# Plain up tiles at the start of each feed-forward stage, and where the norm and the combined inputs are made

## The chip, the cores and the metric

The kernel runs on one core of a Trainium2 chip. The time is the device time of one execution in microseconds (us); three runs of the kernel before gave 2069.99, 2070.28 and 2070.32. One more execution was recorded by the hardware profiler, and all rows below are from it.

## The reference

The input x has 512 tokens of 1024 features in float32. Two blocks follow each other. The kernel computes, in this order: feed-forward stage 0, a mixer with two branches of attention, feed-forward stages 1 and 2, a stick-breaking attention with 16 heads, and feed-forward stage 3. (The second layer type of the reference's second block isn't reached: it has one layer.) Each feed-forward stage is

```
x = x + 0.5 * (silu(gate) * up) @ w_out,   [gate, up] = rmsnorm(x, gain) @ w_in,   w_in: 1024 x (2 * 2816)
rmsnorm(x, g) = x * rsqrt(mean(x * x) + 1e-6) * g
```

Ahead of stage 2 the first block's final norm is applied to x as well, so two norms follow each other there.

## The kernel before, in words

Everything lies with features on the 128 partitions and the 512 tokens along a row, so x is 8 tiles of 128x512. A product in float32 is made of three matmuls of a reduced float32 type: each operand is split into hi (rounded) and lo (the remainder), and hi*hi, hi*lo, lo*hi are added in PSUM. The norm's root is left out of the inputs: xn is x times gain, and the root (rstd) multiplies the results.

Weights come in units of 128x1024 (8 pieces of 128x128) into four slots. SyncE loads a unit, ScalarE rounds it (w_hi, `round_weights`, called ahead by `ahead`), GpSimd makes the remainder (w_lo, `rest`), TensorE multiplies (`unit`, lines 689 to 691, 24 matmuls of 512 columns).

A feed-forward stage n (0 to 3) has 22 up tiles F, each of a gate unit and an up unit; tiles 0 to 11 and 12 to 21 are two chunks c, each followed by its down units, whose results VectorE scales and adds to x. An up tile can be made in two ways. Plain: two units, 48 matmuls of 512 columns. In seven products (Strassen's way, over gate/up, the two halves of the features and the two halves of the tokens): 7 products of 12 matmuls of 256 columns (`product`, lines 766 to 768). The seven need sums of weight quarters (`sum_1` to `sum_4` on VectorE, `copy_c` and `copy_a` on ScalarE, through PSUM), their roundings and remainders (`round_7`, `rest_7`), and combined inputs t of xn: `make_t1` with one operation for each of four features' tiles k, `make_t` with three for each of four j, then rounding on ScalarE (`round_t1`, `round_t`) and remainder on VectorE (`split_t1`, `split_t`); xg is x times gain for them. The products' results are added up on VectorE (`add_p6`, `add_p7_p5`, `add_p4`, `add_p3`), gate gets rstd and silu, and h = up * silu is split.

Before, only stage 0 begins with plain tiles, four of them (PLAIN = 4). Its VectorE makes tile 0, then the combined inputs of k = 0 and 1, then tile 1, and so on (`plain_tiles`). Stages 1 to 3 begin with seven products: `tail_7`, run for each residual tile k as it is updated, rounds and splits the input, makes the combined inputs and adds up squares; `first_products` lets TensorE take products 1, 5, 2 and 6 of tile 0 as their inputs come. The norm's mean is made in tile 1's products, and the first two tiles' gates are kept unscaled until rstd is there (`copied_first`). In stage 2 two means and two roots follow each other (`final_norms`), and cycles F = 2 to 9 scale x by the first norm on VectorE (`x_normed`).

Each engine works off its own list in order, and semaphores hold it back. ScalarE makes the roots by a logarithm and an exponential (`inverse_root`), for which its function table is loaded; silu has another table.

## Time and profile before

| | |
|---|---|
| median of 3 runs | 2070.28 us |
| the profiled execution's own time | 2069.08 us |
| its span, first to last instruction | 2067.3 us |
| TensorE busy | 2017.3 us |
| VectorE, ScalarE, GpSimd busy | 1316.1, 1081.8, 1093.6 us |
| mean granted clock of TensorE | 0.991 of 2.4 GHz |

Busy times overlap between engines, and TensorE's is modelled: a matmul is listed with its own duration although the next one starts before it ends, so its pace is read from counts in a window, not from durations. In the rows PE is TensorE (PEld its weight load), DVE is VectorE, ACT is ScalarE, POOL is GpSimd, SP is SyncE.

### The profile page before, as it was taken

What the parts mean: (1) busy time and instruction counts of PE and PEld (TensorE: products, weight loads), DVE (VectorE), ACT (ScalarE), POOL (GpSimd) and SP (SyncE); (2) the same over time, 40 slices, a digit from 0 to 9 for tenths busy, and PEclk for the clock granted to TensorE, in tenths of its full rate; (3) what the DMA queues carried; (4) which work ended last, traced back from release to release, by engine and by line L of the source; (5) the groups of instructions that cost most, each with busy time, mean ns of one, the idle gap of its engine ahead of it and who ended that gap; (6) DMA issues with size and microseconds to landing.
All of it is one profiled execution on the core that took longest, in us unless ns stands there. A gap on an engine that the chain in (4) does not pass through costs nothing. (4 is left out here: it accounts for less than half of the span.)

```text
span 2067.3 us, 33765 instructions
## 1 busy us (share of the span) xinstructions
PE 2017.3 (98%) x12538; PEld 1782.1 (86%) x12538; DVE 1316.1 (64%) x2312; ACT 1081.8 (52%) x1811; POOL 1093.6 (53%) x728
## 2 busy tenths in 40 slices
PE   8999999999999999999997999999999998999999
PEld 6998998777778889989987998998878877998997
DVE  5762665667763578626677872675688868852762
ACT  6652554344443566525556552564677756642651
POOL 1664775433332458647745674675322335864873
PEclk9999999999999999999999999999999998999999
DMA  4233333322121323332331233223344422332323
GB/s 167 82 103 102 103 101 115 135 82 72 63 71 62 102 72 109 102 107 93 103 112 62 93 100 115 85 97 115 114 133 125 134 82 72 104 107 93 107 96 99
DMA packets 69090, 206.23 MB, mean 100 GB/s; under 512 B 8448, under 2 KB 9472, under 8 KB 68928
## 3 DMA queue, kind: packets, MB, share of 16 engines
q1 hardware_dynamic: 67520, 201.29, 30.3%
q10 hardware_dynamic: 1408, 2.78, 0.4%
q8 instruction: 101, 1.65, 0.3%
q14 instruction: 61, 0.50, 0.1%
HBM read 189.49 MB, written 2.10 MB: 93 GB/s over the span
## 5 line engine op out<-in xcount | busy, mean ns | idle before, releaser
L616 POOL TENSOR_TENSOR w_lo<-raw,w_hi 128x1024 fp32r<-128x1024 f32 (+2 forms) x220 | 442.5, 2022 | 640.4 <-ACT w_hi L1258 475.2
L1258 ACT ACTIVATE w_hi<-raw 128x512 fp32r<-128x512 f32 (+2 forms) x478 | 357.7, 753 | 313.7 <-PE ps L691 250.9
L627 POOL TENSOR_TENSOR w_lo<-s,w_hi 128x512 fp32r<-128x512 f32 x252 | 339.0, 1347 | 195.0 <-ACT w_hi L1258 193.3
L766 PE MATMUL ps<-t_hi,w_hi 128*128 128x256 f32 x1344 | 384.9, 286 | 12.2 <-DVE scratch L1944 6.6
L627 POOL TENSOR_TENSOR w_lo<-raw,w_hi 128x512 fp32r<-128x512 f32 x252 | 324.4, 1299 | 123.4 <-ACT w_hi L1258 123.4
L767 PE MATMUL ps<-t_lo,w_hi 128*128 128x256 f32 x1344 | 382.6, 285 | 0.0
L768 PE MATMUL ps<-t_hi,w_lo 128*128 128x256 f32 x1344 | 382.4, 285 | 0.0
L766 PE MATMUL ps<-xn_hi,w_hi 128*128 128x256 f32 x1008 | 287.7, 285 | 24.3 <-POOL w_lo L627 8.5
L767 PE MATMUL ps<-xn_lo,w_hi 128*128 128x256 f32 x1008 | 287.1, 285 | 0.0
L768 PE MATMUL ps<-xn_hi,w_lo 128*128 128x256 f32 x1008 | 287.1, 285 | 0.0
L766 PEld LDWEIGHTS ps<-t_hi,w_hi 128*128 128x128 f32 x1344 | 260.3, 194 | 16.8 <-DVE scratch L1944 8.1
L767 PEld LDWEIGHTS ps<-t_lo,w_hi 128*128 128x128 f32 x1344 | 260.3, 194 | 0.4
L768 PEld LDWEIGHTS ps<-t_hi,w_lo 128*128 128x128 f32 x1344 | 260.3, 194 | 0.0
L689 PE MATMUL ps<-h_hi_main,w_hi 128*128 128x512 f32 x640 | 249.2, 389 | 0.0
L690 PE MATMUL ps<-h_lo_main,w_hi 128*128 128x512 f32 x640 | 249.2, 389 | 0.0
L691 PE MATMUL ps<-h_hi_main,w_lo 128*128 128x512 f32 x640 | 249.0, 389 | 0.0
L689 PE MATMUL ps<-xn_hi,w_hi 128*128 128x512 f32 x552 | 222.4, 403 | 6.7 <-issue 6.7
L766 PEld LDWEIGHTS ps<-xn_hi,w_hi 128*128 128x128 f32 x1008 | 195.2, 194 | 26.2 <-issue 16.5
L691 PE MATMUL ps<-xn_hi,w_lo 128*128 128x512 f32 x552 | 216.2, 392 | 0.0
L690 PE MATMUL ps<-xn_lo,w_hi 128*128 128x512 f32 x552 | 216.1, 391 | 0.0
L1792 DVE SCALAR_TENSOR_TENSOR ps<-ps,rstd 128x512 f32<-128x512 f32 (+1 forms) x65 | 44.8, 689 | 242.8 <-PE ps L691 242.8
L767 PEld LDWEIGHTS ps<-xn_lo,w_hi 128*128 128x128 f32 x1008 | 195.3, 194 | 0.2
(260 smaller groups left out, 3790.1 us busy)
## 6 DMA issues: line engine op xcount, KB each, us to landing
raw<-weights SPq DMA_DIRECT2D x294, 512.0 KB, 3.2
raw<-weights SPq DMA_DIRECT2D x68, 256.0 KB, 2.8
raw<-weights SPq DMA_DIRECT2D x32, 384.0 KB, 3.0
k_hi_twice<-sb_k_hi SPq DMA_DIRECT2D x31, 128.0 KB, 2.3
k_lo_twice<-sb_k_lo SPq DMA_DIRECT2D x31, 128.0 KB, 2.3
x_sb<-x_t SPq DMA_DIRECT2D x8, 256.0 KB, 6.4
bias<-rel ACTq DMA_DIRECT2D x1, 2048.0 KB, 8.8
q_both<-sb_q_hi SPq DMA_DIRECT2D x16, 128.0 KB, 2.2
```

Source lines behind the costliest of these rows:

```text
L616: nc.gpsimd.tensor_tensor(w_lo[s][:, 0:tiles, :], raw[s][:, 0:tiles, :], w_hi[s][:, 0:tiles, :].bitcast(F32), ALU.subtract).then_inc(S["lo ...
L627: nc.gpsimd.tensor_tensor(quad_of(n, i, w_lo), factor(n, F, i, raw, s_sum), quad_of(n, i, w_hi).bitcast(F32), ALU.subtract).then_inc(S["q_ ...
L689: pe.matmul(to, w_hi[s][:, k, :], hi, start=opens, stop=False)
L690: pe.matmul(to, w_hi[s][:, k, :], lo, start=False, stop=False)
L691: last = pe.matmul(to, w_lo[s][:, k, :], hi, start=False, stop=ends)
L766: pe.matmul(to, w[0][:, k, :], hi, start=opens, stop=False, skip_group_check=True)
L767: pe.matmul(to, w[0][:, k, :], lo, start=False, stop=False, skip_group_check=True)
L768: last = pe.matmul(to, w[1][:, k, :], hi, start=False, stop=(k == QUAD - 1), skip_group_check=True)
L1258: return nc.scalar.activation(dst, src, ACT.Copy)
L1792: return nc.vector.scalar_tensor_tensor(dst, p, scalar, q, ALU.mult, ALU.mult)
```

## The change

Stages 1 to 3 now make tiles 0 and 1 plain and tiles 2 to 11 in seven products; stage 0 keeps its four plain tiles. `first_products`, `opening_cycle`, `tail_7`, `update_7`, `copied_first` and the opening in the tail are gone. The tail squares, rounds and splits each residual tile; for k = 0 to 3 it makes the first combined input of each, and for k = 4 and 5 in stages 1 and 2 (T_IN_TAIL) the three others. The rest of the combined inputs is made behind the tail, as is the norm: the mean comes ahead of the last piece of the first plain unit, ScalarE makes rstd right then, and each plain gate is scaled on its way out of PSUM. ScalarE no longer preloads the logarithm's table in the tail. The first seven-product tile's weights are copied, summed and rounded between plain tiles 0 and 1. In stage 0 the combined inputs of k = 0 and 1 are made ahead of the first gate, and the two first gates follow each other. Stage 2's scaling of x moves from the cycles to the first chunk's down tiles. Between the two chunks, ScalarE's roundings of the next first tile are issued together for k = 6.

```diff
-PLAIN = 4
+PLAIN = [4, 2, 2, 2]
+T_IN_TAIL = [0, 2, 2, 0]
...
-    return PLAIN if n == c == 0 else CHUNKS[c][0]
+    return CHUNKS[c][0] if c else PLAIN[n]
...
+def plain_banks(n, F):
+
+    return [(0, 1), (2, 3), (BANK_OF_2, BANK_OF_2 + 1), (2, 3)][F] if n == 0 else [(weights_bank(n), S2_BANK), (2, 3)][F]
...
+            for u in range(up_unit(n, 0, 0), up_unit(n, PLAIN[n], 0)):
+                if u >= NSLOT:
+                    rest(u)
...
-        def first_products(n, F):
-
-
-            t, p = FFN_INPUT[n], PAIR[n, F]
-            before = FFN_RES[n][0]
-            updated(before - 1, 5)
-            pe.wait_ge(S["xn_lo_done"], DT * t + QUAD)
-            product(n, F, 1)
-            pe.wait_ge(S["t1_lo"], QUAD * n + QUAD)
-            updated(before - 1, 6)
-            product(n, F, 5)
-            pe.wait_ge(S["xn_lo_done"], DT * t + DT - 1)
-            pe.wait_ge(S["p1_copied"], p + 1)
-            product(n, F, 2, (0, QUAD - 1))
-            pe.wait_ge(S["t_lo"], QUAD * n + QUAD - 1)
-            product(n, F, 6, (0, QUAD - 1))
-            pe.wait_ge(S["t_lo"], QUAD * n + QUAD)
-            product(n, F, 6, (QUAD - 1, QUAD))
-            pe.wait_ge(S["xn_lo_done"], DT * t + DT)
-            product(n, F, 2, (QUAD - 1, QUAD))
...
+                if F == first and c == 0:
+                    pe.wait_ge(S["gate_scaled"], FT * n + first - 1)
+                    pe.wait_ge(S["t1_lo"], QUAD * (n + 1))
+                elif F == first:
+                    updated(FFN_RES[n][0], 5)
                 else:
-                    if F == first and c == 0:
-                        pe.wait_ge(S["gate_scaled"], 3)
-                        pe.wait_ge(S["t1_lo"], QUAD)
-                    elif F == first:
-                        updated(FFN_RES[n][0], 5)
-                    else:
-                        pe.wait_ge(S["g1_made"], p)
-                    product(n, F, 1)
-                    if n and c == 0 and F == first + 1:
-                        if n == 2:
-                            mean_squares_final()
-                        else:
-                            mean_square(FFN_STAT[n])
-                    if F >= first + 2:
-                        pe.wait_ge(S["c12_made"], p - 1)
-                    elif F == first + 1 and n == c == 0:
-                        pe.wait_ge(S["gate_scaled"], PLAIN)
-                        pe.wait_ge(S["h_made"], PLAIN)
-                    product(n, F, 5)
-                    if F > first:
-                        pe.wait_ge(S["v2_made"], p)
-                        product(n, F - 1, 4)
-                    if F >= first + 2:
-                        pe.wait_ge(S["c21_made"], p - 1)
-                    if F == first and c == 0:
-                        pe.wait_ge(S["t_lo"], QUAD)
-                    if n == 2 and F == 1:
-                        pe.wait_ge(S["m2_copied"], 1)
-                    product(n, F, 6)
-                    pe.wait_ge(S["p1_copied"], p + 1)
-                    product(n, F, 2)
-                    if F > first:
-                        pe.wait_ge(S["c22_made"], p)
-                        product(n, F - 1, 3)
+                    pe.wait_ge(S["g1_made"], p)
+                product(n, F, 1)
+                if F >= first + 2:
+                    pe.wait_ge(S["c12_made"], p - 1)
+                elif F == first + 1 and c == 0:
+                    pe.wait_ge(S["gate_scaled"], FT * n + first)
+                    pe.wait_ge(S["h_made"], FT * n + first)
+                product(n, F, 5)
+                if F > first:
+                    pe.wait_ge(S["v2_made"], p)
+                    product(n, F - 1, 4)
+                if F >= first + 2:
+                    pe.wait_ge(S["c21_made"], p - 1)
+                if F == first and c == 0:
+                    pe.wait_ge(S["t_lo"], QUAD * (n + 1))
+                product(n, F, 6)
...
+        def plain_tiles(n):
+
+            def one(F, g, waits=None, part=None):
+                u = up_unit(n, F, g)
+                unit(u, u % NSLOT, [plain_banks(n, F)[g]] * UK, xn, waits, part=part)
 
             def first_mean(k):
                 if k == 5:
                     mean_square(S_START)
 
-            first_two()
-            unit(2, 2, [2] * UK, xn)
-            unit(3, 3, [3] * UK, xn, first_mean)
-            tile(2, BANK_OF_2)
-            pe.wait_ge(S["gate_scaled"], 2)
-            pe.wait_ge(S["h_made"], 2)
-            tile(3, 2)
+            if n == 0:
+                first_two()
+                one(1, 0)
+                one(1, 1, first_mean)
+                one(2, 0)
+                one(2, 1)
+                pe.wait_ge(S["gate_scaled"], 2)
+                pe.wait_ge(S["h_made"], 2)
+                one(3, 0)
+                one(3, 1)
+                return
+            waits = first_unit_waits(FFN_INPUT[n], FFN_STAT[n])
+            updated(FFN_RES[n][0] - 1, 1)
+            for g, k0, k1 in ((0, 0, UK - 1), (1, 0, 1), (0, UK - 1, UK), (1, 1, UK)):
+                one(0, g, waits if g == 0 else None, (k0, k1))
+            one(1, 0)
+            one(1, 1)
...
+            elif F == PLAIN[n]:
+                act.wait_ge(S["gate_scaled"], FT * n + F - 1)
...
+        def first_weights(n):
+
+            F = PLAIN[n]
+            copy_c(n, F)
+            round_7(n, F, 1)
+            copy_a(n, F)
+            for i in (5, 6, 2):
+                round_7(n, F, i)
+
+        def plain_tiles(n):
+
+            if n == 0:
+                ahead(2)
+                ahead(3)
+                act.preload_act_table_set("natural_log_exp_and_others")
+                round_sums(S_START)
+                ahead(4)
+                for k in range(QUAD):
+                    make_xg(0, k)
+                root_mean_square(S_START)
+                ahead(5)
+                silu(0, 0)
+                silu(0, 1)
+                round_h(0, 0)
+                round_t1(0, 0)
+                round_t(0, 0)
+                round_h(0, 1)
+                for k in range(1, QUAD):
+                    if k == QUAD - 1:
+                        silu(0, 2)
                     round_t1(0, k)
                     round_t(0, k)
-                if F == PLAIN - 2:
-                    copy_c(0, PLAIN)
-                    copy_a(0, PLAIN)
-                    for i in (1, 5, 6, 2):
-                        round_7(0, PLAIN, i)
+                round_h(0, 2)
+                first_weights(0)
+                silu(0, 3)
+                round_h(0, 3)
+                return
+            u = FFN_BASE[n]
+            round_sums(FFN_STAT[n])
+            ahead(u)
+            first_norm(FFN_STAT[n])
+            ahead(u + 1)
+            if n == 2:
+                second_norm()
+            for j in range(T_IN_TAIL[n], QUAD):
+                round_t(n, j)
+            silu(n, 0)
+            round_h(n, 0)
+            first_weights(n)
+            silu(n, 1)
+            round_h(n, 1)
...
-        def tail_7(k, m):
-
-            t, stat, r = FFN_INPUT[m], FFN_STAT[m], FFN_RES[m][0] - 1
-            act.wait_ge(S["x_updated"], DT * r + k + 1)
-            round_input(k, t)
-            if k < QUAD:
-                nc.scalar.activation(xg[:, k, :], X[:, k, :], ACT.Copy, scale=gains[:, t, k:k + 1])\
-                  .then_inc(S["xg_made"], 1)
-                square(k, k % 2, stat, k)
-                round_t1(m, k)
-                return
-            if k == DT - 1:
-                copy_p1(m, 0)
-            round_t(m, k - QUAD)
-            if k == DT - 1:
-                copy_c(m, 1)
-                round_7(m, 1, 1)
-            square(k, k % 2, stat, k)
-            if k == DT - 1:
-                round_7(m, 1, 5)
-                round_sums(stat)
-            elif k == DT - 2 and m < 3:
-                act.preload_act_table_set("natural_log_exp_and_others")
-
         def tail(k, b, r, t, stat):
             act.wait_ge(S["x_updated"], k + (DT * r + 1))
             square(k, b, stat, k)
             round_input(k, t)
+            if t in FFN_INPUT:
+                m = FFN_INPUT.index(t)
+                if k < QUAD:
+                    make_xg(m, k)
+                    round_t1(m, k)
+                elif k < QUAD + T_IN_TAIL[m]:
+                    round_t(m, k - QUAD)
...
+            if t in FFN_INPUT:
+                m = FFN_INPUT.index(t)
+                if k < QUAD:
+                    make_t1(m, k)
+                    split_t1(m, k)
+                elif k < QUAD + T_IN_TAIL[m]:
+                    make_t(m, k - QUAD)
+                    split_t(m, k - QUAD)
...
-            if n == 2 and 2 <= F < 2 + DT:
-                k = F - 2
-                scale_two(X[:, k, :], X[:, k, :], gains[:, G_FINAL, k:k + 1], scratch[:, 6, :])\
-                    .then_inc(S["x_normed"], 1)
...
+        def split_both(k):
+
+            split_t1(0, k)
+            split_t(0, k)
+
+        def plain_tiles(n):
+
+            if n == 0:
+                for k in range(2):
                     make_t1(0, k)
                     make_t(0, k)
-                    split_t1(0, k)
-                    split_t(0, k)
-                if F == PLAIN - 2:
-                    sums_of_first(0, 0)
-                    rest_of_6(0, PLAIN)
+                dve.wait_ge(S["rstd_ready"], S_START + 1)
+                plain_gate(0, 0)
+                plain_gate(0, 1)
+                make_t1(0, 2)
+                make_t(0, 2)
+                plain_h(0, 0)
+                make_t1(0, 3)
+                make_t(0, 3)
+                split_h(0, 0)
+                plain_h(0, 1)
+                split_both(0)
+                split_h(0, 1)
+                split_both(1)
+                split_both(2)
+                plain_gate(0, 2)
+                plain_h(0, 2)
+                split_both(3)
+                split_h(0, 2)
+            else:
+                split_sums(FFN_STAT[n])
+                for j in range(T_IN_TAIL[n], QUAD):
+                    make_t(n, j)
+                if n == 2:
+                    scale_second_mean()
+                for j in range(T_IN_TAIL[n], QUAD):
+                    split_t(n, j)
+                if n == 2:
+                    both_norms()
+                dve.wait_ge(S["rstd_ready"], FFN_STAT[n] + 1)
+                plain_gate(n, 0)
+                plain_h(n, 0)
+                split_h(n, 0)
+            sums_of_first(n, 0)
+            rest_of_6(n, PLAIN[n])
+            plain_gate(n, PLAIN[n] - 1)
+            plain_h(n, PLAIN[n] - 1)
+            split_h(n, PLAIN[n] - 1)
...
+                if n == 2 and c == 0:
+                    scale_two(X[:, k, :], X[:, k, :], gains[:, G_FINAL, k:k + 1], scratch[:, 6, :])\
+                        .then_inc(S["x_normed"], 1)
+                    dve.wait_ge(S["x_normed"], k + 1)
```

## Rows read from the trace of the kernel before

**Rows 1.** The page: the span and the first row of busy times.

```profile
span 2067.3 us, 33765 instructions
...
PE 2017.3 (98%) x12538; PEld 1782.1 (86%) x12538; DVE 1316.1 (64%) x2312; ACT 1081.8 (52%) x1811; POOL 1093.6 (53%) x728
```

**Rows 2.** Busy time in two undisturbed stretches: matmuls (x) of 512, of 256 columns.

```profile
876.00:934.00 58.00, 58.00 (x258) 48.01 (x257) 13.93 (x21) 14.73 (x21) 27.04 (x16) 1.00 0.30 95
936.00:1032.00 96.00, 96.00 (x802) 96.00 (x802) 68.32 (x128) 59.63 (x112) 74.31 (x58) 1.00 0.31 101
```

**Rows 3.** Busy time (x instructions) by window: stages' starts, later cycles of stage 2.

```profile
27.30:63.05 35.75, 26.61 (x106) 21.11 (x106) 20.37 (x37) 17.98 (x28) 9.09 (x6) 0.90 0.18 59
740.78:866.91 126.13, 121.58 (x988) 120.11 (x986) 97.04 (x169) 82.26 (x148) 93.67 (x72) 0.99 0.29 97
1090.36:1233.95 143.59, 125.58 (x989) 122.63 (x988) 118.07 (x186) 84.86 (x155) 92.88 (x72) 0.96 0.25 84
1703.29:1839.73 136.44, 124.70 (x987) 123.37 (x987) 105.79 (x184) 85.16 (x154) 94.62 (x72) 0.94 0.27 89
1137.00:1215.00 78.00, 72.38 (x591) 71.08 (x591) 67.23 (x106) 44.16 (x84) 53.63 (x42) 1.00 0.28 92
```

**Rows 4.** TensorE in order of time: start, us, instruction [idle before, releaser].

```profile
47.17 0.76 PE L689 MATMUL ps<-xn_hi,w_hi 128*128 128x512 f32 x1 [6.70 <-issue]
...
63.05 0.36 PE L766 MATMUL ps<-xn_hi,w_hi 128*128 128x256 f32 x1 [2.45 <-POOL w_lo L627]
...
747.46 0.36 PE L766 MATMUL ps<-xn_hi,w_hi 128*128 128x256 f32 x1 [3.65 <-ACT scratch L1258]
...
1099.47 0.55 PE L766 MATMUL ps<-xn_hi,w_hi 128*128 128x256 f32 x1 [6.08 <-POOL w_lo L627]
...
1123.11 0.39 PE L766 MATMUL ps<-xn_hi,w_hi 128*128 128x256 f32 x1 [3.68 <-DVE scratch L1971]
...
1148.96 0.39 PE L766 MATMUL ps<-t_hi,w_hi 128*128 128x256 f32 x1 [0.94 <-DVE scratch L1944]
...
1708.62 0.58 PE L766 MATMUL ps<-xn_hi,w_hi 128*128 128x256 f32 x1 [5.17 <-DVE x_sb L2190]
```

**Rows 5.** VectorE, then GpSimd, in order of time, from 1132.5 us.

```profile
1134.01 1.59 DVE L1789 TENSOR_TENSOR scratch<-scratch,rstd 128x512 f32<-128x512 f32 x1
...
1135.53 1.78 DVE L1792 SCALAR_TENSOR_TENSOR x_sb<-x_sb,gains,scratch 128x512 f32<-128x512 f32 x1
...
1132.50 2.55 POOL L627 TENSOR_TENSOR w_lo<-raw,w_hi 128x512 fp32r<-128x512 f32 x2
...
1135.02 1.74 POOL L627 TENSOR_TENSOR w_lo<-s,w_hi 128x512 fp32r<-128x512 f32 x1
```

**Rows 6.** The combined inputs' tile: durations min/median/max in ns.

```profile
L2075 DVE SCALAR_TENSOR_TENSOR t_raw<-x_sb,gains,xg x16: 477/820/1878, 37.6 to 1718.3; 128x256 f32<-128x256 f32 x16
```

**Rows 7.** GpSimd, then VectorE, in order of time, in stage 0's start.

```profile
25.49 9.49 POOL L616 TENSOR_TENSOR w_lo<-raw,w_hi 128x1024 fp32r<-128x1024 f32 x4 [25.05 <-DVE sum_lo L1807]
...
28.94 0.69 DVE L1789 TENSOR_TENSOR scratch<-ps,rstd 128x512 f32<-128x512 f32 x1 [3.25 <-ACT rstd L1322]
...
46.37 0.70 DVE L1789 TENSOR_TENSOR ps<-ps,scratch 128x512 f32<-128x512 f32 x1 [1.18 <-issue]
```

**Rows 8.** ScalarE's groups by form: count, busy us, mean ns.

```profile
L1258 ACT ACTIVATE w_hi<-raw 128x1024 fp32r<-128x1024 f32 x126 | 132.0, 1055 | 153.0 <-PE ps L691 136.3 <-DVE ki L2241 8.0 <-PE ps L768 6.7
...
L1357 ACT ACTIVATE scratch<-x_sb 128x512 f32<-128x512 f32 x40 | 24.8, 621 | 29.9 <-DVE x_sb L2124 29.9
```

**Rows 9.** ScalarE and GpSimd in order of time, before stage 3.

```profile
1687.89 0.72 ACT L1365 ACTIVATE xn_hi<-x_sb,gains 128x512 fp32r<-128x512 f32 x1 [0.29 <-DVE x_sb L2190]
...
1687.68 2.41 POOL L616 TENSOR_TENSOR w_lo<-raw,w_hi 128x1024 fp32r<-128x1024 f32 x1 [8.70 <-ACT w_hi L1258]
```

**Rows 10.** ScalarE in order of time: a table load and the next activation.

```profile
1124.41 1.28 ACT L1403 ACT_TABLE_LOAD   x1
1125.82 0.60 ACT L1403 ACTIVATE ps<-scratch 128x512 f32<-128x512 f32 x1
```

254 lines of the change are left out of this document (79 added, 175 removed).

## The prediction

> **What bounds the kernel now.** I read the page's totals first, then busy time by windows, then TensorE's own list in order of time for what it waited for, then VectorE, ScalarE and GpSimd in the same places. The totals: TensorE is busy 2017.3 of 2067.3 us, so 50 us of idle time is all that better ordering could give back, plus what the lower clock after a pause costs [rows 1]. Two undisturbed stretches give its pace: a matmul of 512 columns every 58.00 / 256 = 0.2266 us, one of 256 columns every 96.00 / 800 = 0.1200 us (two of each count only overlap the edges) [rows 2]. A plain up tile is 48 of the first, 10.88 us; a tile in seven products is 84 of the second, 10.08 us.
>
> The windows at the stage starts show where the loss is [rows 3]. From the last matmul before stage 1 to its eleventh tile lie 126.13 us for 984 matmuls (118.08) and two of the norm's mean (0.45): 7.6 us lost. Stage 2: 143.59 for 118.08 and four of the mean (0.91): 24.6 lost. Stage 3: 136.44, 17.9 lost. In stage 0 the window before the first product holds 105 plain matmuls (23.8 us) in 35.75 us: 11.9 lost. That is 62 us, more than the idle time, because the granted clock is 0.90 to 0.99 of 2.4 GHz there: a pause of 3.65 us or more is followed by matmuls at the 1.2 GHz level. TensorE's waits name the places [rows 4]: 6.70 us for stage 0's first two h tiles; in stages 1 to 3 it waits 3.65, 6.08 and 5.17 us in the first tile's products, since VectorE still works off the last residual tiles with their combined inputs; stage 2 waits again for 3.68 us until the two chained roots are through, then 0.94 us in a later cycle, one of seven such waits. These waits understate: the window over such cycles is 78 us for 589 matmuls (70.7 us), 7.3 us lost [rows 3].
>
> **The change part by part.**
>
> *Six tiles from seven products to plain.* Six times 10.88 - 10.08 = +4.8 us of TensorE, always on the path. The Trainium skill ("TensorE: Matmul & The Clock Gate", Back-to-back issue gap) puts the pace at N / 2.4 GHz + 2.5 ns; that would be 10.36 against 9.17 us a tile and +7.1 us, which speaks more against the change. No row shows that pace; the rows decide.
>
> *What the plain tiles can take back.* In the window of stage 1 two tiles become 96 x 0.2266 = 21.8 us and ten stay (816 matmuls, 97.9 us): 119.7 and the mean. Recoverable, the price already paid: 126.13 - 120.1 = 6.0 us in stage 1; 143.59 - 120.6 = 23.0 in stage 2; 136.44 - 120.1 = 16.3 in stage 3; 11.9 in stage 0, which had four plain tiles already and is only reordered. Sum 57.2 us. What is left of the waits comes off that.
>
> *A cost that the waits don't name.* VectorE's operations with two SBUF inputs and GpSimd's take turns. At 1134.01 a VectorE operation lasts 1.59 us, until 0.55 behind the end of GpSimd's pair; GpSimd's next, started at 1135.02, takes 1.74 us and ends 0.55 before the end of VectorE's next, which takes 1.78 [rows 5]. The first operation of a combined input takes 0.48 us alone and up to 1.88 [rows 6]. So each GpSimd operation holds back one such VectorE operation, and an opening with plain units puts four of 2.41 us [rows 9] there. I count this in every stage. It is what the page "SBUF — State Buffer", Two separate sides, of the Trainium skill calls an exclusive lock; no number here is from there.
>
> *Stage 0.* The eight operations of two combined inputs now stand ahead of the first gate. GpSimd is busy from 25.49 to 34.98 with four remainders [rows 7], so four of the eight wait one out each: 27.9, 30.5, 33.3, 36.0, the others by 38.1 us. The first gate, at 28.94 us now, comes at about 38. Then two gates, eight more combined operations (3.6 us), two h multiplies of 0.70 and a split give the second h tile at 45, against 46.37 + 0.70 now. TensorE pauses at 40.5 for 4.7 instead of 6.70 us, and again has some 2.5 us of half clock. The second wait (2.45, for a first weight remainder) goes: gates, sums and roundings come behind the same h tile, but now with 11 us of plain tile to hide them. Residual 7.8, gain 4.1. Were the turns nothing, the first gate would come at 29.5 and the gain would be 11.9; were GpSimd to hold back all eight, the gain would be -2.
>
> *Stage 1.* Two combined inputs stay in the tail, two move behind it. The last residual update meets a free VectorE, the sums are split 5.5 us behind the last matmul, and the mean stands after 22 plain matmuls (5.0 us) and one more of the other unit (0.7): nothing waits. Weight roundings for the first seven-product tile hang on h of tile 0; I get its first remainders at 760.6 and 762.6 us against TensorE's wish at 763.2 and 764.7. Residual 0.4, gain 5.6. Bounds: 6.0, and 2 if the chain comes 4 us late.
>
> *Stage 2.* The tail has the second sum of squares too; the mean waits about 1.0 us. Then both roots chain: two operations of log and exponential, two multiplies, two more. In this chain stand the two remaining combined inputs and two GpSimd operations, and the splits wait behind the second root on ScalarE. First remainder at 1115.5 (wanted at 1114.1), second at 1117.5, and the first cycle's sums then push the seventh product by 1.4. With 1 us for ripples residual 5.5, gain 17.5. The eight scalings of x (1.78 us each in the cycles [rows 5]) move to the down tiles, where VectorE is busy 13.93 of 58 us [rows 2] and a pair of units lasts 8.2 us: hidden. Without that cover they would cost what they do now, some 9 us. Bounds of the stage: 12 to 23.
> The log's table load is no longer preloaded in the tail. A load takes 1.28 us and the next activation starts 0.13 us behind it [rows 10]; the load runs while ScalarE would wait for the mean, so 0 to 1.3 us. The Trainium skill ("ScalarE: Activation LUTs", What ACT_TABLE_LOAD costs) adds a drain of about 1.38 us; that would make stage 2's gain 16.1. Rows 10 show no such gap.
>
> *Stage 3.* This is the weak place. For the first four tiles ScalarE now squares before it rounds, so the combined difference starts later: square 0.62, round 0.72, product as long, difference and its rounding, about 2.65 us a tile from 1687.89 on, plus a weight rounding of 1.05 [rows 8, 9]. The later four go in strict turns of update, square, round, split: 2.65 us too, though they have no combined inputs any more. With one GpSimd operation in the way I get the inputs of tile 5 at 1709.4, tile 6 at 1712.0, the sums at 1715.3. TensorE is free at 1703.3 and can do tiles 0 to 4: it waits 2.5, 2.0 and 1.9 us. Then four combined inputs with their splits (5.6 + 3.6 us, 4.4 of turns) push the first remainders by 2.3 and the seventh product by 1.3, and the half clock costs 2.7. Residual 12.7, gain 3.6. Without the turns it would be 12, with 4 us more of half clock 0.
>
> *Added waits and queues.* ScalarE's first weight copy now waits for a plain gate, and VectorE's second sum for a plain h; behind the one stand the roundings and silu of tile 1, behind the other the remainder, gate and h of tile 1, and TensorE waits for both. That is the chain I followed above; where it is late, I charged it. SyncE's loads for plain units wait for GpSimd's remainder of the slot's unit, not for six products, so each comes earlier; GpSimd has four remainders of 2.41 us ahead of the first 1.3 us one, done some 10 us before it is due.
>
> *The rest* (bank numbers, the opening of the second halves, loads by the up tile's own slot) moves nothing on the path: the second halves open without a wait now, and 3 us of loads lie far ahead.
>
> **Sum.** 4.1 + 5.6 + 17.5 + 3.6 = 30.8 us off the profiled execution's 2069.08 us (span 2067.3): 2038.3. The median is 1.2 us above that execution; within what this rests on I say 2038.
>
> **The rivals.**
> *Fully hidden* (0.2): the turns and the chains all fit under the plain tiles. For it: GpSimd has few operations in an opening. Against it: rows 5. Stage gains 11.9 + 6.0 + 22 + 12 = 52, time 2017.
> *Late weights everywhere* (0.24): the chain gate, silu, h, rounding, sums, rounding, remainder is serial over three engines; in stage 0 it now ends in a 2.45 us wait [rows 4]. If it is 3.5 us longer than I add up at all four places: 14 us less, 2052. Against it: TensorE has 21.8 us of cover in stages 1 to 3.
> *Slower* (0.03): GpSimd's seven operations of an opening (four of 2.41, three of 1.3 us) each hold back a VectorE operation of the one chain on which h, the rounding and the first product hang; 13.5 us a stage, of which I count about 4.5. All of it would be 36 us more, 2074. It decides from 31 us on, 7.7 a stage. Against it: gates, sums and h read PSUM, and the first gate takes 0.69 us beside a busy GpSimd [rows 7].
> *No change* (0.02): the waits only move behind the plain tiles, by the same amounts.
>
> **How the numbers follow.** The forecast has 0.51. I call within 0.2% (4 us) the same, about what a measurement of this kernel can tell. Range 2018 to 2051: from just above the fully hidden case to most of the late weights. Faster 0.95, same 0.02, slower 0.03.
>
> **What would show it.** Right: plain matmuls of the normed input directly behind stages 1 to 3's last residual matmul; no waits of 0.93 us in stage 2's cycles and the x scalings in the down part at about 0.7 us; the pause at 40 us at 4 to 5 us; a first gate near 38 us; short waits near 1705 to 1716. Wrong: the first gate near 30 us (turns cost less there), or TensorE waiting over 4 us at a first seven-product tile. An undisturbed stage 3 would make it about 10 us faster than I say.

## The result, and the profile after

The changed kernel takes 2038.47 us (median of 4 runs, 2038.09 to 2039.64), the kernel before in the same job 2070.30 (4 runs, 2069.99 to 2071.55). The ratio is 0.9846, with a 95% interval from 0.9829 to 0.9863: 31.8 us less, against a forecast of 2038. The profiled execution has a span of 2036.3 us, 31.0 less than before.

The page's totals, which answer to [rows 1]:

```profile
span 2036.3 us, 33055 instructions
...
PE 2014.3 (99%) x12322; PEld 1769.7 (87%) x12322; DVE 1285.5 (63%) x2245; ACT 1068.1 (52%) x1767; POOL 1074.5 (53%) x704
```

TensorE is busy 3.0 us less although six tiles became 0.8 us dearer each: its mean granted clock is 0.996 instead of 0.991 of 2.4 GHz. Its idle time falls from 50.0 to 22.0 us.

The windows that answer to [rows 3]: from the start of the plain tiles to the first product of the first seven-product tile (stage 0), and from where the matmuls before the stage end to its first down matmul (stages 1 to 3):

```profile
27.30:56.48 29.18, 25.82 (x107) 20.91 (x106) 26.27 (x38) 14.83 (x25) 10.65 (x7) 0.94 0.23 73
733.79:855.14 121.35, 120.43 (x915) 116.24 (x914) 89.26 (x151) 76.94 (x134) 87.10 (x64) 1.00 0.30 101
1078.59:1207.40 128.81, 123.46 (x918) 118.03 (x917) 93.31 (x160) 84.69 (x144) 89.06 (x65) 0.99 0.28 95
1676.73:1808.72 131.99, 125.62 (x916) 118.89 (x915) 98.32 (x167) 80.90 (x142) 86.81 (x64) 0.96 0.27 88
```

The lengths were 35.75, 126.13, 143.59 and 136.44 us. So the gains are 6.6 (7.0 up to the first down matmul), 4.8, 14.8 and 4.4 us: 31.0 in all. The forecast had 4.1, 5.6, 17.5 and 3.6.

TensorE's waits in order of time, which answer to [rows 4]:

```profile
43.94 0.76 PE L696 MATMUL ps<-xn_hi,w_hi 128*128 128x512 f32 x1 [3.36 <-issue]
...
740.31 0.47 PE L708 MATMUL ps<-sum_hi,mean_all_r 128*128 128x512 f32 x1 [0.92 <-DVE sum_lo L1789]
...
1080.83 0.47 PE L696 MATMUL ps<-xn_hi,w_hi 128*128 128x512 f32 x1 [2.08 <-issue]
...
1106.92 0.35 PE L770 MATMUL ps<-xn_hi,w_hi 128*128 128x256 f32 x1 [1.54 <-POOL w_lo L633]
...
1115.13 0.39 PE L770 MATMUL ps<-t_hi,w_hi 128*128 128x256 f32 x1 [1.32 <-DVE scratch L1922]
...
1683.78 0.50 PE L696 MATMUL ps<-xn_hi,w_hi 128*128 128x512 f32 x1 [2.80 <-DVE xn_lo L1818]
...
1686.49 0.80 PE L696 MATMUL ps<-xn_hi,w_hi 128*128 128x512 f32 x1 [1.73 <-DVE xn_lo L1818]
...
1716.47 0.39 PE L770 MATMUL ps<-t_hi,w_hi 128*128 128x256 f32 x1 [0.91 <-DVE scratch L1922]
```

What hung on combined inputs before is gone at the first products; no wait of 0.93 us is left in stage 2's cycles, and 80 us of them (1117.0 to 1197.0) hold 669 matmuls at 0.12 us with TensorE never idle. New is the pause of 2.08 us at 1080.83, in front of the first plain unit of stage 2: its weight remainder was made from 1078.38 to 1080.73, late. Stage 3's waits for its normed inputs are the weak place that the prediction named.

Stage 0's start, VectorE, which answers to [rows 7]:

```profile
25.64 2.03 DVE L2056 SCALAR_TENSOR_TENSOR t_raw<-x_sb,gains,xg 128x256 f32<-128x256 f32 x1 [0.47 <-ACT xg L1396]
27.60 2.62 DVE L2070 SCALAR_TENSOR_TENSOR t_raw<-x_sb,gains,xg 128x256 f32<-128x256 f32 x1
...
32.80 2.50 DVE L2075 SCALAR_TENSOR_TENSOR t_raw<-x_sb,gains,t_raw 128x256 f32<-128x256 f32 x1
35.22 0.47 DVE L2056 SCALAR_TENSOR_TENSOR t_raw<-x_sb,gains,xg 128x256 f32<-128x256 f32 x1
...
36.99 1.28 DVE L1771 TENSOR_TENSOR scratch<-ps,rstd 128x512 f32<-128x512 f32 x2
```

and GpSimd beside it:

```profile
24.98 10.04 POOL L622 TENSOR_TENSOR w_lo<-raw,w_hi 128x1024 fp32r<-128x1024 f32 x4 [24.54 <-DVE sum_lo L1789]
```

Four GpSimd operations, four VectorE operations with both inputs in SBUF at 2.0 to 2.6 us, and the fifth at 0.47: one held back by each, as the prediction counted. The two first gates follow at 36.99.

### The profile page after: what moved, and what is told of

The parts are those of the page before. It is cut to its first block and busy times, and to the rows that moved or that the text cites. A ratio compares the mean times of both kernels' runs of the same rounds, so it can differ in the third digit from the quotient of the medians.

```text
span 2036.3 us, 33055 instructions
## 1 busy us (share of the span) xinstructions
PE 2014.3 (99%) x12322; PEld 1769.7 (87%) x12322; DVE 1285.5 (63%) x2245; ACT 1068.1 (52%) x1767; POOL 1074.5 (53%) x704
## 5 line engine op out<-in xcount | busy, mean ns | idle before, releaser
L622 POOL TENSOR_TENSOR w_lo<-raw,w_hi 128x1024 fp32r<-128x1024 f32 (+2 forms) x232 | 471.8, 2043 | 693.0 <-ACT w_hi L1240 528.3
L633 POOL TENSOR_TENSOR w_lo<-s,w_hi 128x512 fp32r<-128x512 f32 x234 | 312.1, 1335 | 184.8 <-ACT w_hi L1240 183.1
L770 PE MATMUL ps<-t_hi,w_hi 128*128 128x256 f32 x1248 | 353.9, 284 | 2.6 <-DVE scratch L1922 2.2
L771 PE MATMUL ps<-t_lo,w_hi 128*128 128x256 f32 x1248 | 353.5, 283 | 0.0
L772 PE MATMUL ps<-t_hi,w_lo 128*128 128x256 f32 x1248 | 353.5, 283 | 0.0
L633 POOL TENSOR_TENSOR w_lo<-raw,w_hi 128x512 fp32r<-128x512 f32 x234 | 301.7, 1303 | 69.0 <-ACT w_hi L1240 68.9
L696 PE MATMUL ps<-xn_hi,w_hi 128*128 128x512 f32 x648 | 262.3, 405 | 10.3 <-issue 5.4
L770 PE MATMUL ps<-xn_hi,w_hi 128*128 128x256 f32 x936 | 265.3, 283 | 1.5 <-POOL w_lo L633 1.5
L698 PE MATMUL ps<-xn_hi,w_lo 128*128 128x512 f32 x648 | 255.3, 394 | 0.0
L697 PE MATMUL ps<-xn_lo,w_hi 128*128 128x512 f32 x648 | 255.3, 394 | 0.0
```

The costliest lines, as they stand in the source:

```text
L622: nc.gpsimd.tensor_tensor(w_lo[s][:, 0:tiles, :], raw[s][:, 0:tiles, :], w_hi[s][:, 0:tiles, :].bitcast(F32), ALU.subtract).then_inc(S["lo ...
L633: nc.gpsimd.tensor_tensor(quad_of(n, i, w_lo), factor(n, F, i, raw, s_sum), quad_of(n, i, w_hi).bitcast(F32), ALU.subtract).then_inc(S["q_ ...
L696: pe.matmul(to, w_hi[s][:, k, :], hi, start=opens, stop=False)
L697: pe.matmul(to, w_hi[s][:, k, :], lo, start=False, stop=False)
L698: last = pe.matmul(to, w_lo[s][:, k, :], hi, start=False, stop=ends)
L770: pe.matmul(to, w[0][:, k, :], hi, start=opens, stop=False, skip_group_check=True)
```

## The experiments

Twelve kernels ran. Their edits are shown shortened, with words for calls and `...` for what is left out. As times differ by a few us, I also read in each trace how late the first down matmul of every stage comes, and take differences: they show at which stage a microsecond went. Stage 0 is up to that matmul; the others are from one such matmul to the next. Executions with the same stage 0 differ there by up to 1.4 us, and in the later stages by 0.1 (0.4 in stage 3). The interval of a ratio is about 3 us wide to either side, more than the 1.4 to 2.4 us by which single edits of the changed kernel move the median; what is said of these rests on the stage times. The traces are one execution each.

| kernel | time, us | ratio to before | stage 0 | to stage 1 | to 2 | to 3 |
|---|---|---|---|---|---|---|
| before | 2070.3 to 2070.8 | 1 | 141.42 | 725.49 | 367.04 | 605.78 |
| changed | 2038.47 | 0.9846 | 134.39 | 720.75 | 352.26 | 601.32 |
| scalings moved (on before) | 2061.88 | 0.9958 [0.9944, 0.9973] | 142.54 | 725.55 | 358.57 | 606.21 |
| stage 0's order (on before) | 2063.14 | 0.9966 [0.9953, 0.9979] | 135.60 | 725.48 | 367.11 | 605.91 |
| table load at the opening | 2039.83 | 0.9856 [0.9841, 0.9870] | 135.18 | 723.35 | 352.55 | 601.29 |
| no combined inputs in the tail | 2040.07 | 0.9855 [0.9840, 0.9870] | 135.83 | 720.71 | 353.49 | 601.35 |
| table load in the tail | 2038.24 | 0.9845 [0.9829, 0.9861] | 134.82 | 720.76 | 351.57 | 601.33 |
| GpSimd held in stage 0 | 2036.69 | 0.9837 [0.9822, 0.9852] | 132.87 | 720.72 | 352.31 | 601.30 |
| gate ahead of the splits | 2036.35 | 0.9836 [0.9821, 0.9850] | 134.95 | 720.70 | 351.13 | 600.48 |
| updates ahead of the tails | 2036.03 | 0.9834 [0.9820, 0.9849] | 135.47 | 720.75 | 352.28 | 599.15 |
| the four edits | 2031.57 | 0.9809 [0.9795, 0.9822] | 132.87 | 720.76 | 350.42 | 598.24 |
| GpSimd held in 2 and 3 too | 2029.11 | 0.9797 [0.9783, 0.9810] | 132.73 | 720.76 | 348.45 | 597.93 |
| tail of 2 emptied | 2029.06 | 0.9797 [0.9783, 0.9810] | 132.99 | 720.67 | 348.96 | 597.21 |
| norm ahead of inputs 2, 3 | 2029.14 | 0.9800 [0.9786, 0.9813] | 132.45 | 720.71 | 348.48 | 597.92 |

### The scalings of x alone, on the kernel before

```
 cycle(n, c, F):
-    if n == 2 and 2 <= F < 2 + DT:
-        scale_two(X[:, F - 2, :], ...).then_inc(S["x_normed"], 1)
 down(n, c):
     for k in range(DT):
+        if n == 2 and c == 0:
+            scale_two(X[:, k, :], ...).then_inc(S["x_normed"], 1)
+            dve.wait_ge(S["x_normed"], k + 1)
         add_down(n, c, k)
```

> The kernel before with one part of the change alone: the eight scalings of x by the final norm leave the seven-product cycles of stage 2 and stand on VectorE ahead of the eight down updates of the same stage's first half. Theory: in the cycles the scaling is what makes TensorE late (eight cycles of 11.27 us against 10.08), in the down part it hides beside the down matmuls; so cycles of 10.1 us, no TensorE waits of 0.93 us left, and 8 x 1.19 = 9.5 us less: 2070.3 - 9.5 = 2060.8. Rival 1 (the waits would have been filled by something else in the cycle, the turns with GpSimd): half of it or less, 2066 or more. Rival 2 (VectorE in the down part is then late with its updates and TensorE waits for a bank): the gain is given back there, about 2070.

Measured: 2061.88, 8.6 us less; 8.5 of them in stage 2. A window of its later cycles, at full pace:

```profile
1129.60:1209.60 80.00, 80.00 (x669) 80.00 (x668) 61.74 (x113) 51.69 (x98) 62.27 (x48) 1.00 0.33 107
```

The group of the scalings, now in the down part (count, busy us, mean ns, idle before):

```profile
L1792 DVE SCALAR_TENSOR_TENSOR x_sb<-x_sb,gains,scratch 128x512 f32<-128x512 f32 x8 | 9.8, 1224 | 0.0
```

The theory holds, a little short (8.5 of 9.5). They last 1.22 us on the mean (0.74 to 2.72), not the 0.7 that the prediction named, and yet cost nothing there: from this down part's first matmul to that of the next lie 166.12 us, as in the kernel before. So 8.5 of stage 2's 14.8 us have nothing to do with plain tiles.

### Stage 0's order alone, on the kernel before

```
+make_t1/make_t of inputs 0 and 1
 wait rstd
-for F in 0..3: gate F, h F, split F, then two combined inputs with splits (F < 2)
+gate 0, gate 1, input 2, h 0, input 3, split h 0, h 1, splits of the inputs, ...
```

> The kernel before with the order of ScalarE and VectorE in stage 0's plain tiles alone taken from the change. The profile after shows the first seven-product matmul of stage 0 at 56.48 us instead of 63.05. Theory: stage 0 is independent of the other stages' change, so the gain is 6.6 us, of which the prediction had 4.1: 2063.7, with a pause of 3.4 us at 44 us and the first gate at 37 us. Rival: part of the 6.6 us comes from something else in the changed kernel (other weights' order, other waits of TensorE), and the reorder alone gives the 4.1 of the prediction: 2066.2.

Measured: 2063.14, 7.3 us less; in the traces stage 0 is 5.8 us shorter than in the kernel before, the other stages are the same within 0.2. The interval of the ratio is 4.3 to 9.7 us less. So the gain is this order's alone, and above the 4.1 of the prediction by the median and by the stage's time; 5.8 against 7.0 in the changed kernel lies within the scatter of stage 0. The pause was 3.95 us and the first gate came at 37.56, nearly as in the changed kernel.

### The table load at the head of the opening

```
 u = FFN_BASE[n]
+if n < 3:
+    act.preload_act_table_set("natural_log_exp_and_others")
 round_sums(FFN_STAT[n])
```

> The changed kernel with one addition: ScalarE loads the table set with both logarithm and exponential at the start of the openings of stages 1 and 2. Theory: of the four table loads of stage 2's roots three go away; the first logarithm's (1087.78) and the second's (1092.68) lie beside VectorE's chain (which ends at 1095.68), the second exponential's (1096.46, 1.28 us) stands in the chain that ends in TensorE's wait of 1.54 us at 1106.92; stage 1 has no wait and gains nothing. Gain 1.3 to 1.5 us: 2037.1. Rival 1 (each exponential's load is in the chain): 2.6 to 2.9 us, 2035.7. Rival 2 (the loads are hidden altogether, as the prediction's low end had it): nothing, 2038.5.

Measured: 2039.83, 1.4 us slower than the changed kernel: none of the three. ScalarE at the opening of stage 2, then TensorE's wait for the mean in stage 1:

```profile
1089.21 1.28 ACT L1438 ACT_TABLE_LOAD   x1
1090.50 0.63 ACT L1240 ACTIVATE sum_hi<-ssq 128x512 fp32r<-128x512 f32 x1
...
742.17 0.59 PE L708 MATMUL ps<-sum_hi,mean_all_r 128*128 128x512 f32 x1 [2.02 <-DVE sum_lo L1791]
```

I had put the load where it is itself on the path: the rounding of the sums stands behind it, and the mean waits 2.02 instead of 0.92 us in stage 1, with matmuls at a granted clock of 0.61 behind it (742.17 to 746.50). That stage is 2.6 us longer in the profiled execution, which was the slowest of the four (2041.70 us, the others 2039.34 to 2040.03). In stage 2 the mean waits 2.03 us and the clock stays at 1.00. So this run says nothing on what the loads cost; the next one does.

### The table load in the tail

```
 def tail(k, b, r, t, stat):
+    if k == DT - 1 and stat in (S_MIX1, S_FINAL):
+        act.preload_act_table_set("natural_log_exp_and_others")
     act.wait_ge(S["x_updated"], k + (DT * r + 1))
```

> The changed kernel with the table set of logarithm and exponential loaded in the tail, ahead of the last tile's square, where ScalarE waits 1.40 us (stage 2) and 3.65 us (stage 1) for VectorE's update; the run with the load at the head of the opening put its 1.28 us before the rounding of the sums and so before the mean. Theory: no load stands before a mean now and the second exponential's load is out of stage 2's chain; TensorE's wait of 1.54 us at the first seven-product tile shrinks to 0.3 and the stretch from the first plain matmul of stage 2 to its last seven-product matmul is 1.3 us shorter than in the changed kernel: 2037.2. Rival (the loads cost nothing but where they stand before the mean): 2038.5, the wait of 1.54 us stays.

Measured: 2038.24; by the medians no difference, by stage 2's own time 0.7 us less, TensorE's wait at the first seven-product tile 1.11 instead of 1.54. Half of what the theory says. Where the rest went, GpSimd and VectorE show:

```profile
1091.13 2.60 POOL L622 TENSOR_TENSOR w_lo<-raw,w_hi 128x1024 fp32r<-128x1024 f32 x1 [0.40 <-ACT w_hi L1240]
...
1091.51 2.50 DVE L2077 SCALAR_TENSOR_TENSOR t_raw<-x_sb,gains,t_raw 128x256 f32<-128x256 f32 x1
```

With the loads out of the way ScalarE rounds the fourth unit sooner, GpSimd's remainder starts at 1091.13 instead of 1092.74, and holds back an operation of the combined inputs (2.50 instead of 0.48) instead of the mean's scaling (2.17 in the changed kernel, 0.69 here). Counted from VectorE's split of the second sum, the scaling ends 8.9 us later (1087.78 to 1096.70) instead of 8.4 (1087.31 to 1095.68). That eats 0.5 of the 1.28 us of the exponential's load; 0.7 are left.

### No combined inputs in the tail of stage 1's down part

```
-T_IN_TAIL = [0, 2, 2, 0]
+T_IN_TAIL = [0, 2, 0, 0]
```

> The changed kernel with one number changed: in stage 2 no combined input of the second kind is made in the tail of stage 1's down part (two before), all four come in the opening. Theory A (VectorE's backlog in that tail makes the pause of 2.08 us at 1080.83 and the half clock behind it): each of the two costs VectorE 3.3 us in the tail, so without them the last update follows the last down matmul at once instead of 3.7 us late, the pause goes, the mean is ready some 3.7 us earlier, and the two inputs (2.8 us and 1.9 us for the splits) stand in the opening's chain instead: TensorE's wait for the first remainder starts 3.7 us earlier and is longer, net gain 0.5 us, 2038.0. Rival B (the chain of roots is not freed by the earlier mean, the two inputs and splits only lengthen it): 3 to 4.7 us slower, 2041.5 to 2043.2, with a wait of 6 us or more at the first seven-product tile.

Measured: 2040.07, 1.6 us slower; stage 2 is 1.2 us longer. The window in which the plain units begin, without a pause and at full clock:

```profile
1080.00:1086.30 6.30, 6.30 (x29) 5.23 (x28) 5.29 (x9) 4.63 (x7) 0.97 (x2) 1.00 0.27 83
```

TensorE's next wait, at the first seven-product tile:

```profile
1109.49 0.55 PE L770 MATMUL ps<-xn_hi,w_hi 128*128 128x256 f32 x1 [6.64 <-POOL w_lo L633]
```

Both theories have a part in it. VectorE's backlog did make the pause: it is gone with the half clock, the plain units end 3.9 us earlier, counted from the down part's end. But the chain of the roots is now the longer one and gives back 5.1 us: 6.64 us of waiting instead of 3.28 (1.54, 0.42 and 1.32), and the rest because the granted clock is 0.50 in the 5.5 us behind it (1.00 in the changed kernel).

### GpSimd held in stage 0

```
     if u >= NSLOT:
+        if n == 0 and u >= 6:
+            pool.wait_ge(S["t_made"], 6 * (u - 5))
         rest(u)
```

> The changed kernel with two waits added on GpSimd in stage 0: the rests of units 6 and 7 wait until VectorE has made two, and four, of the combined inputs. Theory (turns: a VectorE operation with two SBUF inputs lasts 2.5 us where it falls behind a GpSimd operation, and four of them delay the first gate to 36.99): only two of the operations stay long, the first gate comes at about 33 us, the pause of TensorE at 43.94 (3.36 us) and most of the half clock behind it go, and the first seven-product matmul is 4 to 5.5 us earlier: 2033.0 to 2034.5. Rival (the long operations have another cause, such as ScalarE beside them, and don't follow GpSimd's): they stay at 2.5 us wherever GpSimd stands, 2038.5, or slower if TensorE then waits for units 6 and 7.

Measured: 2036.69, 1.8 us less, 1.5 in stage 0's own time. One such difference is hardly above the scatter of 1.4; but the five runs with this edit have 132.45 to 132.99 us in stage 0, the six with the changed kernel's stage 0 134.39 to 135.83. VectorE, then TensorE:

```profile
33.27 1.28 DVE L1773 TENSOR_TENSOR scratch<-ps,rstd 128x512 f32<-128x512 f32 x2
34.47 1.66 DVE L2058 SCALAR_TENSOR_TENSOR t_raw<-x_sb,gains,xg 128x256 f32<-128x256 f32 x1
...
41.22 1.41 DVE L2064 TENSOR_TENSOR t_lo<-t_raw,t_hi 128x256 fp32r<-128x256 f32 x1
...
54.61 0.39 PE L772 MATMUL ps<-t_hi,w_hi 128*128 128x256 f32 x1 [0.60 <-POOL w_lo L633]
...
60.78 0.39 PE L772 MATMUL ps<-t_hi,w_hi 128*128 128x256 f32 x1 [1.34 <-DVE scratch L1924]
```

The long operations follow GpSimd's: the third and fourth operations of the combined inputs now last 0.42 and 0.48 us (30.64 and 31.10) instead of 2.51 and 2.50, with ScalarE's work beside them as before. So turns are their cause and the rival is out. The first gate comes at 33.27 and the pause shrinks from 3.36 to 0.35 us, as said; the first product comes 4.1 us earlier. But the two held operations take their turns further on (1.66 and 1.41 us), the sums of the first weights come only 1.5 us earlier, and TensorE gives 1.9 us back in two new waits.

### The gate ahead of the combined inputs' splits

```
+if n == 2: both_norms()
+wait rstd; plain_gate(n, 0)
 for j in range(T_IN_TAIL[n], QUAD): split_t(n, j)
-if n == 2: both_norms()
-wait rstd; plain_gate(n, 0)
```

> The changed kernel with one swap on VectorE in the openings of stages 1 to 3: the norm is finished and the first gate scaled before the combined inputs' splits (1.83 us in stage 2, 3.7 in stage 3). Theory (the chain of the roots, gate, h, first weights ends in TensorE's wait of 1.54 us in stage 2): both norms' product comes 2.6 us earlier there, so the wait goes: 1.5 us, and up to 1.3 more if the later wait at 1115.13 goes too: 2035.6 to 2037.0. In stages 1 and 3, where TensorE comes last, nothing. Rival (the splits are then late for the product that reads them): the wait moves to the fourth product of the tile and nothing is gained, 2038.5.

Measured: 2036.35, 2.1 us less: 1.1 in stage 2 and, not expected, 0.8 in stage 3. TensorE at stage 2's first seven-product tile:

```profile
1106.32 0.36 PE L770 MATMUL ps<-xn_hi,w_hi 128*128 128x256 f32 x1 [0.37 <-POOL w_lo L633]
```

The wait is 0.37 instead of 1.54 us; the 1.32 us behind it stay. Not 2.6 us are won in the chain but 1.2, because the h multiply then waits for ScalarE, whose roundings of the inputs and the silu's table load (1098.83 to 1101.69) stand ahead of the silu.

### All updates ahead of stage 3's tails

```
-for k in range(4, DT): update(k, ...) with its tail
+for k in range(4, DT): update(k, ...)
+for k in range(4, DT): wait x_updated; tail(k, k % 2, T_MIX2, S_MIX2)
```

> The changed kernel with one order changed on VectorE ahead of stage 3: the updates of x of tiles 4 to 7 all stand before the tails of these tiles. Theory (the strict turns of update, square, round, split set the 2.7 us per tile, with VectorE idle 0.75 us in each; TensorE waits 0.33, 2.80, 1.73 and 0.60 us for them): with ScalarE ahead a tile takes VectorE 1.3 to 1.4 us, the sums come 3.5 to 4.5 us earlier, TensorE's waits shrink to about 1.5 us in all and stage 3's first seven-product matmul is 4 us earlier: 2034.5. Rival (the chain of combined inputs behind the sums, with two GpSimd operations in it, comes last then): TensorE waits instead for the first remainder at the seven-product tile and at most 1.5 us are gained, 2037.0.

Measured: 2036.03, 2.4 us less, 2.2 in stage 3. VectorE, then TensorE:

```profile
1681.29 2.89 DVE L1818 SCALAR_TENSOR_TENSOR xn_lo<-x_sb,gains,xn_hi 128x512 fp32r<-128x512 f32 x1
1684.10 0.68 DVE L1809 TENSOR_TENSOR ssq<-ssq,scratch 128x512 f32<-128x512 f32 x1
...
1685.36 0.68 DVE L1809 TENSOR_TENSOR ssq<-ssq,scratch 128x512 f32<-128x512 f32 x1
...
1684.23 0.56 PE L696 MATMUL ps<-xn_hi,w_hi 128*128 128x512 f32 x1 [3.42 <-DVE xn_lo L1818]
...
1707.16 0.36 PE L770 MATMUL ps<-xn_hi,w_hi 128*128 128x256 f32 x1 [1.30 <-POOL w_lo L633]
```

A tile now takes VectorE 1.26 us instead of 2.7, as the theory has it, but the first one falls beside GpSimd's operation of 1681.28 and takes 2.89. TensorE waits 3.42 us for normed inputs instead of 5.46, and 1.30 us at the first seven-product tile, where it had not waited: the rival's chain takes over for the rest.

### The four edits together

The edits of the four runs before this one (the load in the tail, not at the opening), unchanged.

> The changed kernel with the four edits of the runs before together: GpSimd's two waits in stage 0, the table load in the tail, the gate ahead of the splits, the updates ahead of stage 3's tails. Theory (they act at four places and add up): 1.8 + 0.2 + 2.1 + 2.4 = 6.5 us less than the changed kernel, 2032.0; the table load may be worth up to 1 us more, since the chain of the roots is shorter by the splits. Rival (TensorE comes last once one of the two stage 2 edits is in, and stage 3's chain is the combined inputs behind the sums whatever the gate does): 4.5 us, 2034.

Measured: 2031.57, 6.9 us less than the changed kernel; 1.5 in stage 0, 1.8 in stage 2, 3.1 in stage 3. They add up, the rival is out.

### GpSimd held in stages 2 and 3 too

```
+if n == 2 and u == FFN_BASE[2] + 2:
+    pool.wait_ge(S["m2_scaled"], 1)
+if n == 3 and u >= FFN_BASE[3] + 2:
+    pool.wait_ge(S["t_made"], 36 + 6 * (u - FFN_BASE[3] - 1))
 rest(u)
```

> As the run with the four edits, with waits on GpSimd in stages 2 and 3 too: stage 2's third unit is not split before VectorE has scaled the second mean, stage 3's third and fourth units not before two and four of the combined inputs are made. Theory (turns): the operations of 2.5 us in the chain behind the sums (1088.4 and 1091.5 in stage 2 of the run with the table load in the tail, 1689.1 and 1692.1 in stage 3 of the run with the updates first) fall to 0.4 to 0.5, and each takes 2.1 us out of the chain; TensorE's waits at the first seven-product tiles, 0.4 and 1.3 us, and the shorter ones behind them (0.4 and 1.3) go in part: 1.5 to 3 us less than the run with the four edits. Rival (a held GpSimd operation only takes its turn from a later one, as in stage 0, where two of four long operations were moved and the chain shortened by 1.5 us instead of 3.7): 0 to 0.5 us less.

Measured: 2029.11, 2.5 us less than with the four edits, 2.0 of it in stage 2. TensorE's waits in stage 2, summed (total, times, longest):

```profile
PE ps L702 <- issue: 2.1, 1, 2.1
PE ps L714 <- DVE sum_lo L1797: 1.0, 1, 1.0
PE ps L702 <- POOL w_lo L622: 0.4, 1, 0.4
```

No first remainder is late any more (the changed kernel waited 2.0 us for these and 1.3 for VectorE). VectorE shows that the turns have not gone but moved, behind the second root:

```profile
1091.90 1.56 DVE L1779 TENSOR_TENSOR rstd<-scratch 128x512 f32<-128x512 f32 x1 [1.46 <-ACT scratch L1320]
...
1094.11 3.31 DVE L2089 TENSOR_TENSOR t_lo<-t_raw,t_hi 128x768 fp32r<-128x768 f32 x2
```

There they lengthen the norm's product by 0.9 us and the splits ahead of h by 1.5. Even so h starts at 1097.34 instead of 1099.71, and the first remainder is ready at 1101.06, 3.0 us before TensorE's first product at 1104.03: the turns fall where there is slack. In stage 3 they fall among inputs and splits of the same chain (2.52 us at 1685.29, and 5.38 instead of 3.55 for the four splits), and only 0.3 us are won: there the rival is right.

### The tail of stage 2 emptied, inputs on both sides of the second mean

```
-T_IN_TAIL = [0, 2, 2, 0]
+T_IN_TAIL = [0, 2, 0, 0]
 VectorE, n == 2:
+inputs 0, 1; scale_second_mean; inputs 2, 3; splits 0, 1; both_norms; gate; splits 2, 3; h
 VectorE, n == 3:
+inputs 0, 1; gate...; inputs 2, 3; splits 0, 1; h; splits 2, 3
```

(With the edits of the run before; ScalarE rounds the inputs in the same order.)

> All edits that helped, and with them stage 2 without combined inputs in the tail (the run that had this alone was 1.6 us slower, with TensorE's pause and half clock behind the down part gone but 6.64 us of wait at the first seven-product tile), now with the second mean scaled after two of its four inputs, ScalarE's rounding of these ahead of the second root, and in stage 3 the gate after two inputs. Theory: the pause of 2.1 us and the half clock behind it (3.9 us in that run) are gained and the chain no longer gives them back: 3.5 to 4 us less than the run with GpSimd held, about 2027. Rival (the chain of two roots and four inputs is still longer than the 22 us that four plain units give it): a wait of 2 us or more at stage 2's first seven-product tile and at most 1.5 us gained.

Measured: 2029.06, the same. The pause is gone, and the plain units end 3.7 us earlier, counted from the last down matmul (2.08 us of pause, 1.01 of the mean's wait, the rest at the edges of the two; there was no half clock to gain, since the granted clock behind the pause is 1.00 in the run with GpSimd held, 1079.18 to 1083.35). But stage 2 is 0.5 us longer, and stage 3 is 0.7 shorter. ScalarE and VectorE in stage 2:

```profile
1087.63 0.63 ACT L1320 ACTIVATE scratch<-scratch 128x512 f32<-128x512 f32 x1
...
1087.16 2.50 DVE L2101 TENSOR_TENSOR t_raw<-t_raw,xg 128x256 f32<-128x256 f32 x1
...
1095.23 0.69 DVE L1785 TENSOR_TENSOR rstd<-scratch 128x512 f32<-128x512 f32 x1
```

The second root is ready at 1088.3, its product is made 7 us later: the order that I wrote put two inputs and two turns (the second at 1089.70) in between. The rival holds in its effect, though the wait at the first seven-product tile is 1.53 us and not 2 or more.

### The norm's product ahead of inputs 2 and 3

```
 VectorE, n == 2:
+inputs 0, 1; scale_second_mean; splits 0, 1; both_norms; gate
+input 2; h; input 3; split h; splits 2, 3
```

(Tail as in the run before; ScalarE rounds inputs 0 and 1 ahead of the second root as there, but input 2 behind the silu and input 3 behind h. The other stages are as in the run with GpSimd held.)

> As the run with GpSimd held (2029.1 us; stages 0, 1 and 3 are its own), with stage 2 in another order: no combined inputs in the tail; in the opening two inputs, the second mean's scaling, the splits of these two, both norms' product and the first gate, and only then the other two inputs, one ahead of h and one behind it, and their splits. The run before it (2029.1 too) had the second root ready at 1088.2 but the norms' product at 1095.23, behind two inputs with two operations of 2.5 us. Theory: the product comes within 1.5 us of the second root, h some 4 us earlier, and the first remainder is ready before the plain units end; no wait of 1.53 us at the first seven-product tile and 1.7 us less behind it: 2025.5 to 2026.5. Rival (the two late inputs and their splits now delay the sums of the first weights as much): 2028.5 to 2029.5, with the wait moved to the third or fourth product.

Measured: 2029.14, the same again. VectorE and GpSimd:

```profile
1086.14 4.00 DVE L2108 TENSOR_TENSOR t_lo<-t_raw,t_hi 128x768 fp32r<-128x768 f32 x2
1090.07 2.88 DVE L1786 TENSOR_TENSOR rstd<-scratch 128x512 f32<-128x512 f32 x1
...
1086.30 6.10 POOL L622 TENSOR_TENSOR w_lo<-raw,w_hi 128x1024 fp32r<-128x1024 f32 x2 [9.45 <-DVE scratch L1786]
```

The product starts at once behind the splits, but splits and product are now the operations with SBUF inputs that stand beside the two held GpSimd operations: 4.00 instead of 1.83 us, 2.88 instead of 0.69. The 4.4 us are what the earlier place was to bring. So three kernels end within 0.1 us of each other, with 348.45, 348.96 and 348.48 us in stage 2; the simplest, with the four edits and GpSimd held, is 41.7 us faster than the kernel before and 9.4 faster than the changed one. Stage 3's order of the run before this one, 0.7 us shorter, was not run together with this stage 2 or that of the run with GpSimd held.

## Why the prediction was right

The total was right to 0.5 us. The mechanism is the one that was told (plain tiles cover the chains, turns and late inputs eat a part of it), but the stages were not as close, and that their errors (+2.9, -0.8, -2.7, +0.8) cancel is luck.

**Stage 0: 4.1 said, 7.0 found.** The mechanism is as told: four turns, first gate at 36.99 (38 said), a pause of 3.36 us (4.7 said), a half clock behind it, no wait for first weights. The gate and what follows it each came about 1 us earlier than I summed, and the residual is 5.4 us (3.36 of pause, the rest at the lower clock), not 7.8 (4.7 and 2.5, and 0.6 for which no term is named); another 0.4 us came in the seven-product tiles. The stage's order alone, on the kernel before, gave 5.8 to 7.3 us; holding GpSimd back moved the gate by 3.7 us, which is the turns' proof.

**Stage 1: 5.6 said, 4.8 found.** "Nothing waits" was wrong by the 0.92 us that the mean waits for the sums' remainder; 0.3 of it is that 24 plain matmuls stand ahead of the mean, 5.4 us and not 5.7. The first remainders were in time, as said.

**Stage 2: 17.5 said, 14.8 found.** The scalings are the largest part: 8.5 us by their own run, by the prediction some 9, hidden in the down part though they last 1.22 us there and not 0.7. The residual is 128.8 - 120.6 = 8.2 us instead of 5.5. The step that failed is what stands ahead of the mean, where the prediction has only "the mean waits about 1.0 us". It left out VectorE's backlog in the tail (the last update 3.7 us late) and with it the first unit's weights, whose rounding stands behind a combined input's on ScalarE: a pause of 2.08 us that it had at nothing. The mean's own 1.0 us was right in size, though this trace doesn't show it: here the lower clock follows the pause (1.7 us lost) and the mean waits for nothing, while in four other runs with the same tail the clock stays up and the mean waits 1.00 or 1.01 us. Stage 2 is as long either way (352.26 here; 352.28 with full clock in the run with the updates ahead of the tails), so the half clock cost nothing on top. In the run with the tail emptied, pause, half clock and the mean's wait are all gone. The other terms held in size: the first remainder late by 1.5 us (1.4 said), the seventh product by 1.3 (1.4 said). What they are made of was not all seen: I charged the logarithm's table load at 0 to 1.3 us and missed that the exponential then wants a set of its own, four loads for the roots instead of one (0.7 us by the run with the load in the tail), and I had not priced the splits that stand ahead of the norm's product (1.1 us by the gate run).

**Stage 3: 3.6 said, 4.4 found.** A tile of the tail took 2.7 to 2.8 us (2.65 said; 3.8 where a turn fell in), TensorE waited 5.5 us for normed inputs and the sums (6.4 said), and the updates run shows that the strict turns of update, square, round and split were the cause. No first remainder was late (2.3 us said), the seventh product by 0.9 us (1.3 said). The half clock was put at 2.7 us; TensorE was busy 125.6 us instead of 120.1, so 5.5 us went there and at the edges of the waits, most of it in two stretches at 0.50 of full clock (1686.49 to 1689.40, and this one):

```profile
1690.02:1695.40 5.38, 5.38 (x13) 4.24 (x14) 5.28 (x5) 3.07 (x5) 4.14 (x2) 0.50 0.27 97
```

So here too two errors cancel: the residual of 11.9 us is close to the 12.7 said because the clock cost 2.8 us more and the waits 3.6 us less. The two are not independent: a slower TensorE comes later to the first remainder. In the run with stage 2's tail emptied the clock is back at 1.00 from 1692.58 on, and there TensorE waits 1.27 us for it (1710.90).

The six plain tiles' price of 4.8 us was not tested by itself. The rivals: fully hidden was ruled out by the pause and the waits above; late weights everywhere by their absence in stages 0, 1 and 3 and 1.5 us in stage 2; slower by the turns being as few as GpSimd's operations, while a gate, which reads PSUM, lasted 0.69 us beside a busy GpSimd (at 1093.50 in the run with GpSimd held).

## What to carry to other kernels

Count one turn for every GpSimd operation that starts while VectorE has operations with both inputs in SBUF to do, and ask which of them stand on the chain: here a turn could be moved to where there is slack, but in no run removed. A change that bundles a reorder with a moved piece of plain work should be taken apart: here the eight moved scalings gave 8.5 of 31 us and needed none of the plain tiles. When a chain is shortened, name the operation that now starts earlier on another engine, and what it meets there. Where a chain of the other engines sets the end of a stage, don't add TensorE's half clock to its waits: what the clock takes, the next wait gives back (stage 2 above).
